# Twelve of the twenty modulation units of layer 0 computed in its latents instead of the opening

## The reference

```python
def trunk_layer(x, mod, lw, lam, l_init, ffn, ctx):
    shift1, scale1, gate1, shift2, scale2, gate2 = jnp.split(mod, 6, axis=-1)
    h = rmsnorm(x, lw['norm_mix']) * (1 + scale1) + shift1
    y, state = token_mixer(h, lw, lam, l_init, ctx)
    x = x + gate1 * y
    h = rmsnorm(x, lw['norm_ffn']) * (1 + scale2) + shift2
    x = x + gate2 * ffn(h)
    return x, state
```

## Time and profile before

| | |
|---|---|
| median of 3 runs | 2237.3 us (2232.9 to 2247.97) |
| the profiled execution | 2244.31 us, of which the span is 2242.4 us |
| TensorE (PE) busy | 1967.8 us, 88% |
| VectorE (DVE) busy | 1420.7 us, 63% |
| ScalarE (ACT) busy | 1040.9 us, 46% |
| mean DMA rate | 168 GB/s |
| mean granted TensorE clock | 0.919 of full |

### The profile page before, as it was taken

The page is one execution under the profiler, slowest core; times in us unless marked ns, Lnnn a source line. Parts: engine busy times, 40 slices in busy tenths (PEclk is TensorE's granted clock), DMA queues, the critical chain, the costliest instruction groups (busy, mean ns, idle before and its releaser), DMA issues.

```text
span 2242.4 us, 28715 instructions
## 1 busy us (share of the span) xinstructions
PE 1967.8 (88%) x11347; PEld 1758.1 (78%) x11347; DVE 1420.7 (63%) x1975; ACT 1040.9 (46%) x1406; POOL 306.4 (14%) x433
## 2 busy tenths in 40 slices
PE   6898578988999999997986689897499999999994
PEld 2798467778999999997986567796378888888883
DVE  1465677434666566655466675434278888888887
ACT  2224476642321121123234566522367777777772
POOL 0035631100011111100074420000100000000001
PEclk9799699979999999998998799897699999999997
DMA  9422000012355555422221000000789999999996
GB/s 383 166 78 85 1 1 1 1 57 76 122 179 169 174 169 184 154 82 62 63 80 34 1 1 1 1 1 1 291 317 386 394 404 395 391 401 391 389 389 229
DMA packets 115911, 375.66 MB, mean 168 GB/s; under 512 B 8640, under 2 KB 66400, under 8 KB 89408
## 3 DMA queue, kind: packets, MB, share of 16 engines
q1 hardware_dynamic: 94448, 303.50, 36.0%
q0 software_dynamic: 14240, 51.49, 6.9%
q10 hardware_dynamic: 7088, 18.81, 2.2%
HBM read 347.13 MB, written 26.64 MB: 167 GB/s over the span
## 4 chain that ended last, share of the span: by engine, by line
PE 73%; DVE 13%; ACT 6%; issue 3%; DMA 3%; POOL 1%; SPq 0%; ACTq 0%; DVEq 0%; POOLq 0%
PE PS L1874 30%; PE PS L1815 24%; PE PS L1854 5%; PE PS L1575 5%; PE PS L1681 4%; DVE NM L1090 2%; ACT E L768 2%; PE PS L1655 2%; DVE SS L1453 1%; DVE NT__176 L1357 1%; DMA raw<-in_w_ada_head 1%; DMA rows_of_slots<-HTM,SLI 1%; ACT PT L775 1%; DMA araw<-in_w_ada_head 1%; PE PS L1736 1%
## 5 line engine op out<-in xcount | busy, mean ns | idle before, releaser
L1874 PE MATMUL PS<-H,split 128*128 128x320 f32 x2688 | 401.7, 312 | 12.3 <-DVE H L1509 10.2
L1874 PEld LDWEIGHTS PS<-H,split 128*128 128x128 f32 x2688 | 400.7, 191 | 13.3 <-issue 13.3
L941 ACT CAST split<-raw 128x2048 fp32r<-128x2048 f32 (+2 forms) x64 | 112.8, 1762 | 269.1 <-PE PS L1874 229.2
L1324 DVE TENSOR_TENSOR split<-raw,split 128x2048 fp32r<-128x2048 f32 (+2 forms) x64 | 138.0, 2162 | 134.5 <-ACT split L941 134.2
L1242 DVE TENSOR_TENSOR split<-raw,split 128x2048 fp32r<-128x2048 f32 x82 | 186.9, 2290 | 51.1 <-ACT split L896 51.1
L1242 DVE TENSOR_TENSOR msplit<-raw,msplit 128x2048 fp32r<-128x2048 f32 x82 | 187.9, 2292 | 32.4 <-ACT msplit L896 32.4
L1815 PE MATMUL PS<-split,HT 128*128 128x512 f32 x816 | 198.6, 400 | 5.5 <-DVE HT L1221 5.5
L1815 PE MATMUL PS<-msplit,HT 128*128 128x512 f32 x816 | 190.5, 389 | 0.0
L1090 DVE TENSOR_REDUCE NM<-PS 128x1 f32<-128x640 f32 (+1 forms) x180 | 123.6, 714 | 104.7 <-PE PS L1655 104.4
L896 ACT CAST msplit<-raw 128x2048 fp32r<-128x2048 f32 x82 | 156.8, 1914 | 64.4 <-PE PS L1815 64.4
L896 ACT CAST split<-raw 128x2048 fp32r<-128x2048 f32 x82 | 157.2, 1917 | 61.0 <-PE PS L1815 45.7
(11 more groups left out here) (291 smaller groups left out, 2985.5 us busy)
## 6 DMA issues: line engine op xcount, KB each, us to landing
raw<-in_moe_w_gate SPq DMA_DIRECT2D x55, 1024.0 KB, 7.2
raw<-in_moe_w_down SPq DMA_DIRECT2D x55, 1024.0 KB, 7.8
raw<-in_moe_w_up SPq DMA_DIRECT2D x54, 1024.0 KB, 6.9
DOTW<-in_w_ada_rows POOLq DMA_DIRECT2D x56, 512.0 KB, 4.4
mraw<-in_moe_w_up SPq DMA_DIRECT2D x14, 1024.0 KB, 6.7
mraw<-in_moe_w_gate SPq DMA_DIRECT2D x13, 1024.0 KB, 7.3
mraw<-in_moe_w_down SPq DMA_DIRECT2D x13, 1024.0 KB, 7.9
raw<-in_w_ada_head SPq DMA_DIRECT2D x12, 1024.0 KB, 18.4
```

The costliest lines, as they stand in the source:

```text
L941: A.copy(split[u % 2][:, 0, 0:w], src[:, 0:w]).then_inc(S["split_hi"], 1)
L1324: V.tensor_tensor(split[u % 2][:, 1, 0:w], src[:, 0:w], split[u % 2][:, 0, 0:w].bitcast(f32), ALU.subtract).then_inc(S["split_lo"], 1)
L1874: ins = T.matmul(PS[:, 4 * (u % 2) + 2 * c + hf, 0:HALF], W[:, w, k, c * P:(c + 1) * P], A[:, a, k, hf * HALF:(hf + 1) * HALF], start=(k = ...
```

## The change

The opening computes 8 units (4 blocks: shift1 and scale1). The other 12 units (6 blocks: gate1, shift2, scale2) are loaded into the slots `raw[0]` to `raw[2]`, which the last three `w_in` units leave free, and multiplied in the latents of layer 0, two per tile.

All blocks of a part now gather in one bank, 6, instead of two alternating ones: COND is a window of 42 columns with the two vectors in one place and zeros around them, and each block takes another 32 columns of it, so that its two rows land in rows of their own and all others add zero. There is one copy of the rows, one turn and one bias addition for each part (SEL has up to 12 columns), instead of ten. The second part's window and its rows lie in `raw[3]`. SP holds back the `w_out` loads until the second part is turned. The first bank's modulation is waited for with `mod_ready` 1 by the first norm, 2 by the second.

x is loaded first, ahead of the units, and its squares, sums and 1/rms are made in one piece beside the units. The casts of the first two weight units move into the loop that makes H.

```diff
+EARLY_BLOCKS = 2 * D_MODEL // ADA_COLS
+LATE_BLOCKS = ADA_BLOCKS - EARLY_BLOCKS
+A_RAW, LATE_RAW = 2 * EARLY_BLOCKS, 3
+WINDOW = STRIP + 2 * (max(EARLY_BLOCKS, LATE_BLOCKS) - 1)
...
         @block.sync
-                    sp.wait_ge(S["ada_used"], N_ADA // A_RAW * A_RAW + n + 1)
+                    sp.wait_ge(S["ada_used"], n + 1)
...
-            for j in range(3):
-                head(j)
+            for k in range(0, KC, KC // 2):
+                sp.dma_start(xT[:, k:k + KC // 2, :], I["x_chunks"][:, k:k + KC // 2, :]).then_inc(S["x_loaded"], 16)
             sp.dma_start(VEC[:, :, :], I["vectors"]).then_inc(S["vec_loaded"], 16)
-            for j in range(3, N_ADA):
...
-                head(j)
+            for j in range(A_RAW):
+                modulation(j, araw[j]).then_inc(ada_in[j], 16)
...
+                if l == 0:
+
+                    for j in range(N_ADA - A_RAW):
+                        i = j % LATE_RAW
+                        if j < LATE_RAW:
+                            sp.wait_ge(S["split_lo"], n - LATE_RAW + i + 1)
+                        else:
+                            sp.wait_ge(S["late_used"], j - LATE_RAW + 1)
+                        modulation(A_RAW + j, raw[(n - LATE_RAW + i) % RAW_SLOTS]).then_inc(late_in[i], 16)
+                    sp.wait_ge(S["mod_turned"], 2)
                 w = chunks(I["w_out"][l])
...
         def mixer_act(...):
                 root(HEADS, QK)
 
+
+            if l == 0:
+                rows_out(1)
...
         @block.scalar
+            def rows_out(i):
+                if i == 0:
+                    act.wait_ge(S["ada_used"], A_RAW)
+                else:
+                    act.wait_ge(S["late_used"], N_ADA - A_RAW)
+                A.copy(ROWS[i], PS[:, 6, :]).then_inc(S["mod_rows_out"], 1)
 
             act.wait_ge(S["eps_ready"], 1)
-            rows_out(0)
+            act.wait_ge(S["x_loaded"], 32)
+            for k in range(KC):
+                A.activation(XSQ[:, k, :], xT[:, k, :], ACT.Square).then_inc(S["sq_ready"], 1)
             act.wait_ge(S["lam_summed"], 1)
             A.activation(LTMP[:, :], LTMP[:, :], ACT.Exp).then_inc(S["lam_exp"], 1)
...
-            split_hi(0)
             act.wait_ge(S["x_mean"], 1)
             A.activation(XROOT[:, :], XMEAN[:, :], ACT.Sqrt).then_inc(S["x_root"], 1)
-            rows_out(ADA_BLOCKS - 1)
-            split_hi(1)
+            rows_out(0)
+            split_hi(0)
...
                     for kc in range(KC):
+                        if q == 0 and kc == 2:
+                            split_hi(1)
...
         def mixer_dve(...):
+            if l == 0:
+                condition(1)
             turned_lo(0)
...
+                if l == 0 and k == -1:
+                    modulation_out(1)
+                    gain(0, 1)
+                    dve.wait_ge(S["mod_ready"], 2)
...
         @block.vector
+            def condition(i):
+                z = COND[i]
+                n = (EARLY_BLOCKS, LATE_BLOCKS)[i]
+                if i:
+                    dve.wait_ge(S["split_lo"], U_LATENT + 1)
+                V.memset(z, 0.0).then_inc(S["cond_ready"], 1)
+                dve.wait_ge(S["cond_ready"], 2 * i + 1)
+                V.tensor_copy(z[:, :, 2 * n - 2:2 * n], CSIL).then_inc(S["cond_ready"], 1)
...
+            condition(0)
             lambda_sums()
+            for k in range(KC):
+                x_acc(0, k)
             lambdas()
+            x_mean(0)
+            x_rstd(0)
             dve.wait_ge(S["vec_loaded"], 16)
...
+            modulation_out(0)
+            gain(0, 0)
+            dve.wait_ge(S["mod_ready"], 1)
...
                             ins.then_inc(S["hm_ready"], 1)
+                        if q == 0 and kc in (1, 4):
+                            split_lo(kc // 4)
...
         def mixer_pe(...):
                 if t + 1 < KT_TILES:
                     turn_c(t + 1)
+                if l == 0:
+                    late_unit(2 * t)
+                    late_unit(2 * t + 1)
                 pe.wait_ge(S["ct_lo"], l * KT_TILES + t + 1)
...
             for g in range(6):
                 turn_group(0, g)
+            if l == 0:
+                rows_turn(1)
...
+                    if l == k == 0:
+                        pe.wait_ge(S["ada_out"], 2)
...
         @block.tensor
+            def modulate(i, j, n, W):
+
+                b, last = j // 2, n // 2 - 1
+                first = 2 * (last - b)
+                W = W[:, :].rearrange("p (k n) -> p k n", k=KC // 2)
+                for k in range(KC // 2):
+                    ins = T.matmul(PS[STRIP * k:STRIP * (k + 1), 6, :], COND[i][:, 4 * (j % 2) + k, first:first + STRIP],
+                                   W[:, k, :], start=(j == 0), stop=(j == n - 1))
+                return ins
+
+            def rows_turn(i):
+                n = 2 * (EARLY_BLOCKS, LATE_BLOCKS)[i]
+                pe.wait_ge(S["mod_rows_out"], i + 1)
                 for c in range(4):
-                    ins = T.matmul(PS[:, 7, 2 * c:2 * c + 2], ROWS[:, b % 2, c * P:(c + 1) * P], SEL[:, :],
-                                   start=True, stop=True)
+                    ins = T.matmul(PS[:, 7, c * n:(c + 1) * n], ROWS[i][:, c * P:(c + 1) * P], SEL[:, 0:n], start=True,
+                                   stop=True)
                 ins.then_inc(S["mod_turned"], 1)
+
+            def late_unit(j):
+                if j == 0:
+                    pe.wait_ge(S["cond_ready"], 4)
+                pe.wait_ge(late_in[j % LATE_RAW], 16 * (j // LATE_RAW + 1))
+                slot = (U_LATENT - LATE_RAW + j % LATE_RAW) % RAW_SLOTS
+                modulate(1, j, N_ADA - A_RAW, raw[slot]).then_inc(S["late_used"], 1)
...
+            for j in range(A_RAW):
+                if j == A_RAW // 2:
+                    x_sum(0)
+                pe.wait_ge(ada_in[j], 16)
+                modulate(0, j, A_RAW, araw[j]).then_inc(S["ada_used"], 1)
+            rows_turn(0)
             x_rows(0)
```

118 lines of the change are left out of this document (37 added, 81 removed).

## The result

| | median (range), executions | against the kernel before on the same chip |
|---|---|---|
| before | 2235.49 us (2232.9 to 2247.97), 4 | |
| the change | 2209.42 us (2203.82 to 2214.28), 4 | ratio 0.9868, 95% interval 0.9837 to 0.9899 |
| the change, once more | 2208.13 us (2206.94 to 2215.41), 6 | ratio 0.9865, 95% interval 0.9843 to 0.9888 |

The forecast was 2206.5 us in a range of 2197 to 2221 and "faster" at 0.80. The kernel is 26 to 33 us faster by the medians of the two comparisons (2235.49 and 2241.11 us for the kernel before), against 30.7 forecast.

What follows compares the result with a forecast made beforehand. Full DMA engines bound the opening, VectorE the loop of layer 0's latents. -34.5 + 3.8 = -30.7 us took the profiled 2244.3 us to 2213.6; the median, 7.0 lower, gave 2206.5, range 2197 to 2221.

Steps and rivals of the forecast that it cites:

- The opening: Stretch before layer 0's first product: twelve fewer loads ahead of it were to gain 34.5 us.
- the two bounds: Limits of the opening's gain by TensorE's clock: 37 us if fast, 31 if slow to reach full speed.
- the fast bound: Opening: unit, turn and spreading at TensorE's faster speed, 2.9 us more gained, 37 in all.
- slow sum: Opening: chain counted at TensorE's slower speed, first product starting at 46.2 instead of 82.26 us.
- the third rival: Opening gives less: statistics of x come 8 to 10 us later, -22 in all, 2215 us; chance 0.08.
- The latents: Layer 0's six tiles with two units each, loads and tail included: 3.8 us lost, ends about +1 and +8.
- tile 1's: First tile of layer 0's latents: two units ahead of its products cost +1 us, ends -0.5 and +2.5.
- the warm clock: Rival: units filling the latents' gaps raise TensorE's clock, 3 us more gained behind the loop, 2203.5 us; chance 0.10.
- some 17 of 20: Latents' loop: TensorE's busy time with the added units, in us of a 20 us stretch, before 9.70.
- The tail: Behind the latents' loop: ScalarE's copy +0.56, TensorE's turn +1.2, VectorE's bias and gain +0.7 us; 2.5 together.
- Units not hidden: Rival in the latents: 23.3 us of units plus the 2.5 tail come back, net -8.7, 2228.6 us; chance 0.12.
- The ring of slots: Rival in the latents: nine late loads each exposed for 5.4 us, 48.6 in all, net +17.9, 2255 us; chance 0.04.

Runs made afterwards that it cites:

- both: The change with weight unit 1's low half split behind the H loop and the late rows turned among the score turns: 2203.84 us, 0.9834 against the kernel before.

## Why the prediction was right, and where it was not

**The opening: right, with a spread between the two bounds.** Forecast 34.5 at the copy of UU (its step by step sum gave 34), measured 36.5, and 37.0 between the second profiles. Each step up to unit 8 stood: landing forecast at 33.8, multiplied at 34.13. From there the chain took 9.8 us instead of 12.4, 1.9 of the 2.6 being the turn (1.06 for 1.84) and the spreading (1.36 for 2.48): the fast bound that the prediction had named and not taken. The slow one was not wrong: ten profiles here have this opening, and in them the product starts at 43.55 to 46.50 us; three start at 46.19 or later, with turn and spreading at 1.88 and 2.48 us, where the prediction's slow sum says 46.2. The statistics of x were no wait (TensorE summed the squares at 25.31 us, directly behind unit 4), so the third rival is out. The split of weight unit 1 was put at 2.2 us. From the product's start to UU it is 17.74 us instead of 15.89 and 16.27, so the price was 1.5 to 1.9 us, and 1.15 of it goes away when the split is moved behind the loop; TensorE holds the rest.

**The latents: the mechanism right, the size too large.** Forecast +3.8 us, measured -0.2 at the first scores and +0.8 at the third item. The term that was mis-sized is tile 1's: "a TensorE kept busy could win 1.2 back. Ends -0.5 and +2.5, I take +1", with 0.3 more for tile 2. The two units put tile 1's products 0.35 us later, and these take 1.5 us less, so tile 1 ends 1.2 us early; by the turn of QS it is 1.1 us early, where the forecast had 1.3 late. The units ran at the fast figure and not near the slow one, and the fast products directly behind them, which the prediction named, came in full. What the prediction says of the other tiles stood: their products shorten too (4.7 us over all tiles), hidden behind VectorE. I had set the warm clock aside as a rival of 0.10 that helps behind the loop. It was granted in the loop (0.94). Behind the loop, where the rival put its 3 us, the clock was 0.50 as before and nothing was won. The "some 17 of 20" us of TensorE was too high: in the stretch that answers to it, 208.2 to 228.2 us, it was busy 10.8 of 20 at 0.86. The Trainium skill (TensorE: Matmul & The Clock Gate, What's actually happening) has a low clock as the default, released by activity; 0.94 in the filled loop and 0.50 in the gaps behind it agree with that.

**The tail: right in sum.** ScalarE's copy +0.5 for +0.56, TensorE's turn +0.7 for +1.2, VectorE +0.6 for +0.7, and a longer stretch at the lower clock, for which there was no term; in all 2.2 by the version that moves it, forecast 2.5. The distance from the first product to the first scores, forecast at 201 to 204 us, was 198.8 in both profiles of the change: the first product took 1.85 us more than before, as above, and the way from UU to the scores 0.2 less.

**The rivals.** Units not hidden: out, 0.1 us per unit. The ring of slots: with three it costs 0.4 to 0.8 us, with one 30; the forecast had the mechanism and the condition right, and its cover of 1 to 3 us per load was what the run with one slot took away.

**The sum.** By the anchors the change is 35.7 us ahead at the third item (298.40 and 262.75), 36.3 between the second profiles, where the forecast had 30.7: 2 us of the difference are the opening, 2.4 the tiles, the rest smaller terms. Behind that point nothing is given back: at the end of the span the two profiles of the change are 40.5 and 36.7 us ahead of the first profile of before. The medians show less, 26 and 33 us, because of the executions that the change is set against. The profiled execution of before took 3.5 us more than the median of 47 executions, 2240.8, and 33 is the difference by that median; the 26 rest on four executions of before with a median of 2235.49. So the forecast of the total was near partly by luck: it was 2 us too low in the effect (30.7 for 33, and 5 by the anchors), and it started from a median of three, 2237.3, that was 3.5 us too low. It also knew nothing of what the clock does in the attentions, whose length varies by up to 16 us over the profiles. Whether the change gets the lower clock there more often than the kernel before is not shown: layer 0's attention took 213.2 us in both its profiles, before 211.4 and 218.8.

## What to carry to other kernels

Work on an engine with waits is nearly free when it is spread over the waits in pieces of about their size, and costs its loads' full time when it stands together: with the same twelve units the way from UU to the scores is 181.06 us spread and 209.70 together. A higher clock on such an engine is worth only what the engine's path shows: 4.7 us of shorter products, 1.1 us of time. The loads of the spread work need as many slots as make the wait between use and next landing shorter than the stretch between two uses; with one slot in place of three a load per tile stood exposed. And read an edit at anchors (a named instruction near the edit, ahead of it and behind it) and not from the total alone: here the total scatters by 12 us between executions while the distance between two anchors repeats within 0.3 us (181.23 and 181.47, 181.06 and 181.10, 180.24 and 180.01).

## What the runs showed of the hardware

- The time of an execution follows how long TensorE is granted the lower clock. In the attentions the time at the lower level and the length of the stretch were, read from the profiles: 30.1 us and 207.6, 35.6 and 209.7, 40.7 and 211.4, 45.9 and 213.2, 57.5 and 217.9, 59.1 and 218.8, 76.7 and 223.5: about 0.35 us for each us. Of the 26 attentions in the profiles the one furthest from a straight line through all stands 1.1 us off it (`both`, layer 0: 43.1 and 213.5). The ten executions of the change show the same over the whole kernel: 2203.82 us at a mean granted clock of 0.928 and 2215.41 at 0.921, which are 317 and 350 us at the lower level by the spans, and 11.6 us of time.
- Less work can be slower by this: two units left ten of twelve units out, its loop had the gaps of before again, and it lost 10 us in the attention of layer 0, where two more stretches of 17.1 us at the lower clock stood. That the gaps in the loop caused these stretches was not shown; the kernel before shows stretches of 17.1 us there without any edit, one in its first profile and two in its second.
- Units of 32 columns directly behind products of full width, and the reverse, left no gap that the trace shows: 0.96 us per MB of weights at the higher clock, 1.94 at the lower, and the next product starts at once (185.53 behind 183.68 and 1.92).
- One core moved 410 GB/s from memory while all 16 DMA engines were full. The Trainium skill (Perfetto Trace Analysis, Roofline) puts the practical ceiling of a single core at about 120% of 358 GB/s; the 410 of this trace are 115%.
